# A hybrid decoder layer with a mixture of experts: loads, transposes and splits issued in another order

## What is computed

```python
xn = rms_norm(x, g_mix);  u = xn @ w_in                      # 1664 columns, split in six
y_lru = rg_lru(conv(u_lru)) * gelu(u_gate)                   # 384 wide recurrence
y_swa = sliding_window_sink_attention(q, k, v, sinks)        # 6 heads, 2 kv heads, window 128
mkv = rms_norm(mem, g_mem) @ w_mem_kv                        # 256 memory tokens
y_mem = memory_cross_attention(qm, km, vm)                   # 4 heads
h = x + concat(rms_norm(y_lru), rms_norm(y_swa), rms_norm(y_mem)) @ w_out
xt = rms_norm(h, g_ffn)
gates, experts = softmax(top4(xt @ w_router + b_router))     # 32 experts
out = h + sum over the 4 experts e of gate * (clamped_swiglu(xt @ w1[e] + b1[e]) @ w2[e] + b2[e])
```

## Time and profile before

| what | value |
|---|---|
| median of three runs | 2336.19 us |
| the profiled execution, its own time | 2335.18 us |
| its span in the profile | 2333.5 us |
| TensorE busy | 2178.6 us, 93% of the span |
| VectorE busy | 1402.2 us, 60% |
| ScalarE busy | 1050.4 us, 45% |
| GpSimd busy | 259.7 us, 11% |
| moved by DMA | 477.62 MB |
| first loop pass starts at | about 624 us |

### The profile page before, as it was taken

How to read it: one execution, slowest core, us unless ns; L and a number is a source line. 1 busy time by engine, 2 the same in 40 slices (tenths; PEclk the granted TensorE clock), 3 DMA queues, 4 the chain that set the end, 5 groups by cost and what they waited for, 6 DMA issues and landing times.

```text
span 2333.5 us, 30095 instructions
## 1 busy us (share of the span) xinstructions
PE 2178.6 (93%) x9748; PEld 1612.8 (69%) x9749; DVE 1402.2 (60%) x1809; ACT 1050.4 (45%) x1253; POOL 259.7 (11%) x202
## 2 busy tenths in 40 slices
PE   6999688997699999999999999999999999999997
PEld 4443477544378877786687878787767877887885
DVE  4140566333686568667766665767877557557565
ACT  3231254011364456545645454545655445445444
POOL 2000300001111111101101010101111101002001
PEclk9999888898799999999999999999999999999998
DMA  7000400201597669968959585858988668558556
GB/s 250 0 0 0 171 1 1 90 28 39 216 330 253 203 196 353 327 184 312 356 204 307 195 300 190 297 180 310 350 321 289 191 194 286 177 197 301 184 184 222
DMA packets 202149, 477.62 MB, mean 205 GB/s; under 512 B 14727, under 2 KB 19911, under 8 KB 202048
## 3 DMA queue, kind: packets, MB, share of 16 engines
q1 hardware_dynamic: 184622, 437.95, 52.4%
q0 software_dynamic: 17424, 39.17, 7.2%
q10 hardware_dynamic: 66, 0.02, 0.0%
HBM read 468.73 MB, written 32.11 MB: 215 GB/s over the span
## 4 chain that ended last, share of the span: by engine, by line
PE 64%; DVE 11%; issue 8%; ACT 7%; DMA 7%; DVEq 1%; POOLq 1%; ACTq 0%; POOL 0%; SPq 0%
PE ps L1077 13%; PE ps L1079 13%; PE ps L1078 13%; PE ps L852 7%; DMA out<-y,idx_cur 6%; PE ps L1002 5%; DVE w_lo L1543 5%; ACT w_hi L729 3%; PE ps L1112 1%; PE ps L1130 1%; PE ps L1134 1%; DVE hm L1605 1%; PE ps L956 1%; DVE onehot L1532 1%; PE ps L1071 1%
## 5 line engine op out<-in xcount | busy, mean ns | idle before, releaser
L1543 DVE TENSOR_TENSOR w_lo<-ring,w_hi 128x2048 fp32r<-128x2048 f32 x349 | 796.6, 2288 | 337.0 <-ACT w_hi L729 336.7
L729 ACT ACTIVATE w_hi<-ring 128x2048 fp32r<-128x2048 f32 x346 | 655.5, 1915 | 381.8 <-PE ps L1079 355.5
L1077 PE MATMUL ps<-w_hi,xT_hi 128*128 128x512 f32 x1288 | 512.7, 398 | 26.7 <-ACT y L755 15.5
L1079 PE MATMUL ps<-w_hi,xT_lo 128*128 128x512 f32 x1288 | 503.6, 391 | 0.0
L1078 PE MATMUL ps<-w_lo,xT_hi 128*128 128x512 f32 x1288 | 503.1, 391 | 0.0
L1077 PEld LDWEIGHTS ps<-w_hi,xT_hi 128*128 128x128 f32 x1288 | 242.6, 188 | 88.1 <-issue 27.5
L1077 PE MATMUL ps<-w_hi,actT_hi 128*128 128x512 f32 x720 | 289.3, 402 | 0.0
L1079 PE MATMUL ps<-w_hi,actT_lo 128*128 128x512 f32 x720 | 281.9, 392 | 0.0
L1078 PE MATMUL ps<-w_lo,actT_hi 128*128 128x512 f32 x720 | 281.2, 391 | 0.0
L1078 PEld LDWEIGHTS ps<-w_lo,xT_hi 128*128 128x128 f32 x1288 | 242.2, 188 | 55.4 <-issue 4.5
L1079 PEld LDWEIGHTS ps<-w_hi,xT_lo 128*128 128x128 f32 x1288 | 242.2, 188 | 51.6
(11 more groups left out here) (261 smaller groups left out, 1998.5 us busy)
## 6 DMA issues: line engine op xcount, KB each, us to landing
ring<-in_w SPq DMA_DIRECT2D x390, 1024.0 KB, 5.8
xh<-in_x SPq DMA_DIRECT2D x4, 2048.0 KB, 20.7
work<-in_w_out SPq DMA_DIRECT2D x1, 4096.0 KB, 13.9
token_rows<-uT POOLq DMA_DIRECT2D x8, 512.0 KB, 2.9
out<-xh SPq DMA_DIRECT2D x8, 512.0 KB, 2.7
work<-in_w_in SPq DMA_DIRECT2D x2, 1536.0 KB, 17.5
uT<-in_w_mem_kv SPq DMA_DIRECT2D x1, 2048.0 KB, 17.8
ring<-in_w_in SPq DMA_DIRECT2D x2, 1024.0 KB, 17.2
```

The source lines that it names most:

```text
L729: act_e.activation(w_hi[s % SPLIT][:, :, :], slot(s), ACT.Copy).then_inc(hi_ready, counted(s, whole))
L1077: pe.matmul(acc, hi, whi, start=first, stop=False)
L1079: return pe.matmul(acc, lo, whi, start=False, stop=last)
L1543: return dve.tensor_tensor(lo, x, hi.bitcast(F32), ALU.subtract)
```

## The change

Six edits of order, in five engines' programs:

1. SP loads `w_mem` ahead of the first half of x, in place of behind it.
2. SP issues the four key copies ahead of the load of `w_out`, with the same waits for each.
3. TensorE projects the memory ahead of `x_transposes(0)`, and does `x_transposes(1)` between units 2 and 3.
4. Ahead of the loop, GpSimd in place of VectorE makes the remainders of slots 0 to 2, behind its first gather and ahead of its wait for `init_out`.
5. In each pass, one group or two, VectorE does `take_alo(2)` ahead of the split of slot 11.
6. In each pass, one group or two, ScalarE does `combine(0)` ahead of the split of slot 14.

```diff
--- before.py
+++ after.py
@@ -325,8 +325,8 @@
             load_vectors(sp, 0)
             sp.dma_start(mem_sb, mem[0].rearrange("(t p) d -> p t d", p=P)).then_inc(mem_in, 16)
             xv = x[0].rearrange("(t p) d -> p t d", p=P)
+            sp.dma_start(w_mem, w_mem_kv[0].rearrange("(k p) c -> p k c", p=P)).then_inc(w_mem_in, 16)
             sp.dma_start(xh[:, 0:4, :], xv[:, 0:4, :]).then_inc(x_in[0], 16)
-            sp.dma_start(w_mem, w_mem_kv[0].rearrange("(k p) c -> p k c", p=P)).then_inc(w_mem_in, 16)
             sp.dma_start(xh[:, 4:8, :], xv[:, 4:8, :]).then_inc(x_in[1], 16)
             wv = w_in[0].rearrange("(k p) c -> p k c", p=P)
             def load_wA(i):
@@ -336,9 +336,6 @@
             for i, (a, b) in enumerate(((384, 640), (0, 384), (640, 896))):
                 sp.dma_start(wB[:, :, a:b], wv[:, :, 768 + a:768 + b]).then_inc(wB_in[i], 16)
             load_wA(1)
-
-            sp.wait_ge(in_done, len(units))
-            sp.dma_start(w_out_sb, w_out[0].rearrange("(k p) c -> p k c", p=P)).then_inc(wout_in, 16)
 
             sp.wait_ge(normed, norm_units.index((1, 0)) + 1)
             sp.wait_ge(kz_zero, 5)
@@ -346,6 +343,8 @@
                 for half in range(2):
                     sp.dma_start(kz[g][half][half * DH:(half + 1) * DH, :],
                                  uT[g * DH:(g + 1) * DH, K, :]).then_inc(kz_in, 16)
+            sp.wait_ge(in_done, len(units))
+            sp.dma_start(w_out_sb, w_out[0].rearrange("(k p) c -> p k c", p=P)).then_inc(wout_in, 16)
             sp.wait_ge(spread, len(norm_units))
             sp.wait_ge(scanned, LT)
             for i in range(2):
@@ -497,6 +496,9 @@
 
             po.wait_ge(idx_ready, 1)
             gather_x()
+            for s in range(LEAD):
+                po.wait_ge(hi_ready, s + 1)
+                po.tensor_tensor(w_lo[s][:, :, :], slot(s), w_hi[s][:, :, :].bitcast(F32), ALU.subtract).then_inc(raw_done[s], 1)
             po.wait_ge(init_out, 16 * NT)
             po.memset(no_index[:, :], 0).then_inc(zeroed, 1)
             po.wait_ge(zeroed, 5)
@@ -771,8 +773,8 @@
                     if len(groups) == 1:
                         take_xhi(p + 2, 0, next_x_bank(groups))
                     split_hi(13)
+                    combine(0)
                     split_hi(14)
-                    combine(0)
                     combine(1)
 
                 with act_e.If(two > 0):
@@ -814,7 +816,6 @@
                         m = pe.transpose(ps[:, b, t * P:(t + 1) * P], xs[:, t, k * P:(k + 1) * P], ident[:, :])
                     m.then_inc(tr_done, 1)
 
-            x_transposes(0)
             pe.wait_ge(w_mem_in, 16)
             pe.wait_ge(tr_out, 4)
             pe.wait_ge(vec_ready, 1)
@@ -827,7 +828,7 @@
                         m = pe.matmul(ps[:, u, 0:MEM], memT_v[:, k, (u - 2) * P:(u - 1) * P], w_mem[:, k, MEM:2 * MEM],
                                       start=k == 0, stop=k == KD - 1)
                 m.then_inc(mkv_done, 1)
-            x_transposes(1)
+            x_transposes(0)
 
             def unit(i):
                 h, c = units[i]
@@ -886,6 +887,8 @@
                           rroot[:, h * HALF:(h + 1) * HALF], start=True, stop=True).then_inc(spread, 1)
 
             for i in range(8):
+                if i == LT:
+                    x_transposes(1)
                 unit(i)
             for c in range(LT):
                 gate_products(c)
@@ -1566,9 +1569,6 @@
                 dve.wait_ge(init_mm, u + 1)
                 hh = xh[:, i, half * HALF:(half + 1) * HALF]
                 dve.tensor_tensor(hh, ps[:, 2 + u % 2, :], hh, ALU.add).then_inc(init_ready, 1)
-            for s in range(LEAD):
-                dve.wait_ge(hi_ready, s + 1)
-                minus_hi(w_lo[s][:, :, :], slot(s), w_hi[s][:, :, :]).then_inc(raw_done[s], 1)
             take_xlo(1, 0, 4)
             dve.wait_ge(b1_hi, 1)
             minus_hi(b1w[E:2 * E, :], b1_raw[E:2 * E, :], b1w[E:2 * E, :]).then_inc(b1_lo, 1)
@@ -1650,9 +1650,10 @@
                         if j == 3:
                             if len(groups) == 2:
                                 take_xlo(p + 2, 0, next_x_bank(groups))
-                            split_lo(11)
                         if j:
                             take_alo(j - 1)
+                        if j == 3:
+                            split_lo(11)
                         split_lo(2 * j + 6)
                         if j == 1:
                             make_onehot(p + 2)
```

## The result

| | before | after |
|---|---|---|
| median | 2335.85 us (4 runs beside it) | 2367.01 us (4 runs, 2364.25 to 2371.61) |
| ratio, 95% interval | | 1.0137 [1.0121, 1.0153] |
| span of the profiled execution | 2333.5 us | 2366.1 us (own time 2367.85) |
| mean granted TensorE clock | 0.974 | 0.971 |

What follows compares the result with a forecast made beforehand. One-group passes were taken as bound by a ring through combine, scatter, `idx_cur` and VectorE; TensorE is hardly idle in two-group passes. Terms -4.8 - 7.5 - 4.2 + 6.8 + 4.0 = -5.7 us gave 2331 us, range 2318 to 2343.

Steps and rivals of the forecast that it cites:

- Two-group passes get the same order in the code: Loop, two-group passes: the second pair of combines starts 0.31 us later, 13 x 0.31 = +4.0 us.
- ScalarE's hold is paid twice: Rival, loop: combine ahead of slot 14's split delays both pass kinds; +12.4 us, 2349 us; chance 0.13.
- The port pair: Rival, first softmax: VectorE blocks for whole GpSimd instructions, so key copies give -2.4 in place of -7.5; 2336 us; chance 0.08.
- The 1.9 us that I took off: First softmax: VectorE slowed beside GpSimd in two or three stretches, cutting the key copies' gain from -9.4 to -7.5 us.
- The prelude, -4.8: Start of kernel: memory projection ahead of x's transposes starts the fourth unit at 65.6 in place of 70.4, -4.8 us.
- three units are ... 20.6: Prelude: TensorE's three units ahead of the second transposes take 20.6 us, to 59.5.
- The entry, -4.2: Loop's entry: three remainders go to GpSimd, so the first `sel` comes at 624.8 in place of 629.05, -4.2 us.
- One-group passes, +0.36: Loop, one-group passes: the second `combine` comes later and lengthens the ring by 0.36 us, 19 x 0.36 = +6.8 us.
- the three signs that I named: Loop, profile after: no TensorE wait for `y` at L1077, new waits for `actT_lo` before slot 11 and `sel` before L1130.
- TensorE alone: Rival, loop: TensorE alone bounds the passes and its waits go, a further 34.1 us, 2286 us; chance 0.06.
- the front's -16.5: Ahead of the loop: prelude -4.8, key copies -7.5 and entry -4.2, together -16.5 us.
- the loop's +10.8: Loop: one-group passes +6.8 us and two-group passes +4.0 us.

Runs made afterwards that it cites:

- e4_one_group: The changed kernel with the combine(0) edit kept in one-group passes only: 2328.14 us, 0.9984 of the kernel before.
- both doses: Kernel before plus dummy VectorE steps, two-input or one-input control: behind every `sel`, 2370.48 and 2363.28 us; behind two-group passes, 2343.39 and 2337.44 us.
- e2_alo: The kernel before with only take_alo(2) moved ahead of the split of slot 11: 2322.92 us, 0.9948.
- the first dose: Kernel before plus two dummy VectorE steps behind `sel` in every pass: 2370.48 us with two SBUF inputs, 2363.28 us with one as control.
- e3_front: The change without its two reorderings inside the passes (parts 5 and 6): 2319.46 us, 0.9942 of the kernel before.

## Why the prediction was wrong

**The step that failed: "Two-group passes get the same order in the code".** I put the second pair of combines 0.31 us later and priced that at 4.0 us; the pair came 0.3 us late as said, and the part cost 34.2 us. That is 30 of the 36 us by which the forecast was off. What I did not follow was the other thing that part 6 moves there: VectorE's remainder of slot 14. It goes 3.9 us back, onto the scatters' issues. I did have the 3.9 us, in the rival "ScalarE's hold is paid twice", but asked only whether `sel` would be late. It was, by the 1.0 us named (0.9), and that is not what costs. What costs is GpSimd: 0.8 us at the first issue (at 1037.17 the running step had 0.9 left, to 1038.10), 1.6 at the second (at 1039.90 it had 1.8 left, to 1041.67), 1.6 more to the landing, 0.3 for the pair, together the 4.4 of the trace.

This accounts for the whole cost. Against `e4_one_group`, which differs in this order alone, `idx_cur` comes 34.5 us later over the eight seams and A is 34.2 us longer; seam by seam the two agree to 0.4 us but for one, where 4.1 of 5.0 us arrive. The first two sizes follow from the rule that both doses show. The 1.6 us of the landing I can't place: loads of weights move 300 GB/s during the second issue, 100 before. It goes with the late issue and not with part 6 as such, since at the seam that was late in the kernel before the landing took 9.12 us too; no run tells whether the loads make it.

**The port pair.** I had it as a rival, at the first softmax, where VectorE would be the one to wait (0.08). The Trainium skill (SBUF — State Buffer, "SBUF: two separate sides") calls the pair an exclusive lock that blocks the loser for the whole instruction. In the loop it does just that, with GpSimd as the loser: an issue waits for the end of a two-input step. At the softmax it does not show as such: beside GpSimd's work VectorE's copies took 1.01, 0.28 and 0.96 us, and began where another had not ended:

```profile
272.22 1.01 DVE L1350 COPY ring<-ring 128x256 f32<-128x256 f32 x1
273.48 0.28 DVE L1350 COPY ring<-ring 128x256 f32<-128x256 f32 x1
274.01 0.96 DVE L1350 COPY ring<-ring 128x256 f32<-128x256 f32 x1
...
271.12 3.70 POOL L456 TENSOR_SCALAR uT<-uT,vecs 128x1024 f32<-128x1024 f32 x1
274.81 1.91 POOL L454 TENSOR_TENSOR work<-uT 128x1024 f32<-128x1024 f32 x1
```

The first copy ended within a GpSimd step; the third ended 0.2 us behind the start of the next one. The copy of 0.28 us lay within a GpSimd step as well, here and in the kernel before (282.27, beside a step that ran to 283.60), so no trace shows that GpSimd is what lengthens the others. The 1.9 us that I took off for it were not needed: with the copies alone the first softmax starts at 271.48, where the forecast had 271.4, and the kernel is 12.8 us faster (9.6 to 16.1), where -9.4 was its best end. What lies beyond 9.4 no run places.

**The prelude, -4.8.** By the median of the prelude alone, 5.1 us, the size was about right; in the change's own trace it is missed, and this is where. The start of the projection was right (18.93 for 18.9), and so was the second pair of transposes and copies (63.20 to 69.29, the 6.1 forecast). Unit 0 came at 39.46 in place of 38.9, because ScalarE's copies of the projection stand behind a square root that waits for VectorE. What failed is "three units are ... 20.6" and everything behind it at the pace of the earlier trace rows: I priced all of TensorE's work at the full clock, though the new order puts three idle stretches of 1.0 to 2.6 us into a part that had run without any. The units took 3.1 us more and what follows 69.29 another 1.7. In the trace of the prelude alone the three units took 20.7 us, as forecast, and the gain was 1.7 us here; in the change's it is a loss of 0.8.

**The entry, -4.2.** Right by the trace; no run has this part alone. GpSimd's three took 13.49 us (13.1 forecast), `sel` is 3.0 behind the remainder of `b1w`, and between ScalarE's first split and `sel` there are 32.1 us in place of 36.2:

```profile
590.27 13.49 POOL L501 TENSOR_TENSOR w_lo<-ring,w_hi 128x2048 fp32r<-128x2048 f32 x3
615.77 0.29 DVE L1626 TENSOR_TENSOR sel<-ident 128x128 fp32r x1 [3.01 <-issue]
```

**One-group passes, +0.36.** From one `idx_cur` to the next it is 40.6 in place of 40.1 between one-group passes, near the forecast 40.5, and the three signs that I named (new waits for `sel` and `actT_lo`, none for `y`) came. But the net hid two sizes: part 5 gives 10.4 us (A and B of `e2_alo`), part 6 takes 17.8, so that 7.4 are left against the +6.8 of the sum. What TensorE could have done without it, 38.6 us, I had put aside under "TensorE alone".

Of the sum, the front's -16.5 came out at -13.3, the loop's +10.8 at +39.5 to the last token-id products.

## What to carry to other kernels

When a step is moved on one engine, follow every consumer's new time and lay it over what the other engines do there, not only over who waits for it: here the harm was that a VectorE step with two SBUF inputs came to run when GpSimd had to issue its scatter. Ask at each seam what is started by GpSimd and what VectorE runs at that moment; a VectorE idle stretch at such a place may be what keeps the transfer short. And test an edit in each kind of pass apart: its text was the same in both, its cost 1.8 us in one and up to 5.2 in the other.

## What the runs showed that I had not expected

- GpSimd's issue of an indirect DMA, 1.6 us by itself, waits for the end of a VectorE step with two SBUF inputs that is running, by 0.5 to 1.8 us in the rows above; it doesn't for a reduction with one input, and not for a step that starts after it.
- The granted clock can fall to half behind an idle stretch of TensorE of 1.5 us, in a loop that is otherwise busy, and needn't: after, it did so behind 3 of the 31 waits for `sel` and 2 of the 9 for `act` (2.5 and 2.6 us), in `e4_one_group` behind 5 of 18 waits for `sel`. Behind the wait shown here matmuls take 0.63 us that take 0.39 elsewhere (the second row is a window's: us, busy time by engine, clock, DMA share, GB/s).

```profile
1083.10 0.64 PE L1133 MATMUL ps<-b1w,sel 128*128 128x512 f32 x1 [1.46 <-DVE sel L1626]
...
1084.00:1086.00 2.00, 2.00 (x6) 1.61 (x5) 2.00 (x3) 0.08 (x1) 0.00 (x0) 0.50 1.07 398
```

- In the prelude alone the projection ran at half its pace (9 matmuls from 19 to 23 us, 19 in the change) while the records gave a clock of 1.00. Either the clock's column missed a slow stretch or something else held the matmuls; no run tells, but their number shows the stretch.
- The same code ran at different granted clocks in different executions: attention (260 to 400 us) at 0.89 in the kernel before and at 0.93 in the first dose, which has the same code up to the loop, and ScalarE's root at its end came at 416.12 and 408.20. The first `sel` lies anywhere from 622.22 to 630.71 in the seven profiled executions with the front of the kernel before, so a size of the front read from two traces, as my 13.3 us, is uncertain by some us; by the medians `e3_front` gives 13.5.
